# Hybrid encoder layers: sliding attention in units of one chunk and two heads per group, f32r scores, rotary swaps by transfers, the mix split by token chunk

## What is computed

```python
u = rmsnorm(h, norm_g)
sb_q, sb_k, sb_v, sb_g, sw_q, sw_k, sw_v, sw_g = split(u @ w_in)       # 1024 x 3328
sb_o = stick_breaking_attention(sb_q, sb_k, sb_v) * silu(sb_g)         # 8 heads of 64, causal
qr, kr = rope(sw_q), rope(sw_k)                                        # 8 query heads, 2 key heads
sw_o = sliding_window_gqa(qr, kr, sw_v, sinks) * silu(sw_g)
h = h + concat(sb_o, sw_o) @ w_out                                     # 1024 x 1024
```

## Time and profile before

| | us |
|---|---|
| three runs, median | 1393.2 |
| lowest, highest | 1391.79, 1398.45 |
| profiled execution, its own time | 1392.5 |
| its span | 1390.7 |

### The profile page before, as it was taken

How to read it: one execution, slowest core, us unless ns; L and a number is a source line. 1 busy time by engine, 2 the same in 40 slices (tenths; PEclk the granted TensorE clock), 3 DMA queues, 4 the chain that set the end, 5 groups by cost and what they waited for, 6 DMA issues and landing times.

```text
span 1390.7 us, 23502 instructions
## 1 busy us (share of the span) xinstructions
PE 1274.6 (92%) x9314; PEld 1162.3 (84%) x9314; DVE 819.4 (59%) x1560; ACT 450.9 (32%) x1239; POOL 235.3 (17%) x96
## 2 busy tenths in 40 slices
PE   4699999999898999979979999999989899997996
PEld 3598888988787888869969898888878788886995
DVE  5926555464766777652392664546475677765327
ACT  4313333233243333331131333333324333333113
POOL 1421111011010010232142111011101101023211
PEclk7699999999999999989999999999999999997998
DMA  4511110111001110031311111011100010103103
GB/s 160 192 46 31 31 32 16 31 31 32 16 17 23 25 24 24 31 123 47 138 61 46 31 31 29 19 31 31 27 21 16 16 31 16 32 31 120 50 16 121
DMA packets 96075, 64.24 MB, mean 46 GB/s; under 512 B 35920, under 2 KB 89424, under 8 KB 95968
## 3 DMA queue, kind: packets, MB, share of 16 engines
q1 hardware_dynamic: 94960, 61.22, 14.6%
q10 hardware_dynamic: 864, 1.35, 0.3%
q0 software_dynamic: 144, 0.18, 0.1%
HBM read 50.21 MB, written 12.71 MB: 45 GB/s over the span
## 4 chain that ended last, share of the span: by engine, by line
PE 75%; DVE 15%; issue 5%; ACT 3%; POOL 1%; DMA 0%; SPq 0%; DVEq 0%; ACTq 0%; POOLq 0%
PE psum L605 34%; PE psum L610 16%; PE psum L661 6%; PE psum L690 5%; PE psum L673 5%; DVE dvT L1172 3%; DVE mix L1068 2%; PE psum L726 2%; DVE X L1248 2%; PE psum L754 1%; PE psum L728 1%; PE psum L757 1%; DVE small L1245 1%; PE psum L722 1%; PE psum L739 1%
## 5 line engine op out<-in xcount | busy, mean ns | idle before, releaser
L605 PE MATMUL psum<-UH,WH 128*128 128x344 f32 (+1 forms) x1632 | 548.5, 336 | 21.2 <-DVE UL L1075 8.3
L605 PE MATMUL psum<-UL,WH 128*128 128x344 f32 (+1 forms) x1632 | 532.8, 327 | 0.0
L610 PE MATMUL psum<-UH,WL 128*128 128x344 f32 (+1 forms) x1616 | 523.9, 324 | 0.4 <-POOL WL L1358 0.4
L605 PEld LDWEIGHTS psum<-UH,WH 128*128 128x128 f32 x1632 | 314.9, 193 | 40.0 <-issue 15.6
L1358 POOL TENSOR_TENSOR WL<-w_raw,WH 128x1024 fp32r<-128x1024 f32 x68 | 174.2, 2563 | 1024.1 <-DVE WH L1116 1024.1
L605 PEld LDWEIGHTS psum<-UL,WH 128*128 128x128 f32 x1632 | 314.4, 193 | 0.4
L610 PEld LDWEIGHTS psum<-UH,WL 128*128 128x128 f32 x1616 | 309.4, 191 | 1.4 <-POOL WL L1358 1.4
L1193 DVE TENSOR_TENSOR_SCAN X<-X,stick 16x16 f32<-16x16 f32 (+5 forms) x144 | 123.9, 903 | 29.6 <-ACT X L956 29.4
L966 ACT ACTIVATE PT<-psum 128x512 f32<-128x512 f32 (+6 forms) x328 | 130.9, 440 | 22.3 <-PE psum L673 11.4
L956 ACT ACTIVATE X<-psum 128x264 f32<-128x264 f32 (+9 forms) x240 | 91.2, 432 | 82.8 <-PE psum L661 82.6
L1196 DVE TENSOR_TENSOR_SCAN X<-X 128x352 f32<-128x352 f32 (+4 forms) x96 | 94.7, 1027 | 29.5 <-ACT X L956 29.5
(11 more groups left out here) (129 smaller groups left out, 1498.1 us busy)
## 6 DMA issues: line engine op xcount, KB each, us to landing
w_raw<-in_w_in SPq DMA_DIRECT2D x36, 512.0 KB, 3.7
h_spill<-X SPq DMA_DIRECT2D x16, 520.0 KB, 5.1
X<-h_spill SPq DMA_DIRECT2D x16, 520.0 KB, 5.2
w_raw<-in_w_in SPq DMA_DIRECT2D x32, 256.0 KB, 3.7
w_raw<-in_w_out SPq DMA_DIRECT2D x16, 256.0 KB, 2.8
w_raw<-in_w_out SPq DMA_DIRECT2D x32, 128.0 KB, 3.3
out<-X SPq DMA_DIRECT2D x6, 512.0 KB, 4.2
mix<-in_x SPq DMA_DIRECT2D x3, 512.0 KB, 5.6
```

Of the source, the lines that this page charges most:

```text
L605: pe.matmul(bank[:, 0:width], WH[:, j % 2, k, :], u[:, k, chunk_uses(c)], start=(k == 0 and u is UH), stop=False)
L610: ins = pe.matmul(bank[:, 0:width], WL[:, j % 2, k, :], UH[:, k, chunk_uses(c)], start=False, stop=(k == KT - 1))
```

## The change

- **Units.** Sliding attention goes by 18 units (`UNITS`): half hp (two query heads of each group) and range r (two chunks of 64 tokens; one unit for the meta tokens). Within a unit, query columns are ordered by chunk and head, 128 of them for one chunk and two heads, against exactly 144 keys (meta, chunk before, own chunk), laid out in `SKH`, `SKL` as 16 groups of 80 columns. There is no mask.
- **Scores** are three f32r products each (queries and keys split in high and low), each of 64 partitions, one group on each half; both score banks belong to one unit.
- **Rotary.** ACT copies the projection to `dvT`, SP swaps the halves by four SBUF to SBUF transfers into `vT`, DVE has three operations on 128 partitions, one task later; high parts (ACT) and low parts (POOL) come another task later.
- **Order.** Values first, then `sk`, `sq 0`, `sq 1` fill the fourth stick stage; then `sg 0`, `sg 1`, `sq 2`, `sq 3` and, in the second nine units, `sg 2`, `sg 3`. A unit's steps are ST (main and meta part), SZ of n+2, SAV of n-1, SD of n+1.
- **Mix.** `split` goes by token piece and by rows (0 to 3 with POOL's low part, 4 to 5 and 6 to 7 with DVE's). Gates of half 0 are applied where DVE reads the values; half 1 is gated by piece. Two output products of the first piece are made ahead of SAV 14 and SAV 16 (`EARLY_OUTS`); their addition is a step of its own.
- **Pieces** are 400, 384 and 256 tokens. Reloads of `h` start by row as rows come free. The values' projection and the half-1 gates need no factor 0.5 any more; it is in the copy of the values.

```diff
-CHUNKS = [(0, 352), (352, 344), (696, 344)]
+CHUNKS = [(0, 400), (400, 384), (784, 256)]
-P_RING = 4
-REST_RING = 4
+P_RING, P_SLOT = 3, 688
+REST_RING = 3
...
-WEIGHT = dict(Z=1.5, T=0.6, R=0.0, AV=0.6, AV_rest=0.15, SZ=1.0, SD=0.3, ST=0.7, SAV=0.5, gate=0.0)
-OUT_ORDER = [0, 2, 1, 3, 4, 5, 6, 7]
+WEIGHT = dict(Z=1.0, T=0.6, R=0.0, AV=0.6, AV_rest=0.15, SZ=0.7, SD=0.0, ST=0.4, SAV=1.0, gate=0.0, split=0.0)
+OUT_ORDER = [4, 5, 6, 7, 2, 3, 0, 1]
+EARLY_OUTS = {(0, 0): ("SAV", 14), (1, 0): ("SAV", 16)}
+META_UNIT = 8
+UNITS = [(hp, r) for hp in range(2) for r in (0, META_UNIT, 1, 2, 3, 4, 5, 6, 7)]
+HALF = len(UNITS) // 2
...
+    def delayed(tasks):
+        out = [list(task) for task in tasks] + [[], []]
+        for i, task in enumerate(tasks):
+            for step in task:
+                if step[0] == "proj" and ORDER[step[1]][0] in ("sk", "sq"):
+                    e = rope_tile(*ORDER[step[1]][:2])
+                    out[i + 1].append(("rope_add", e, step[2]))
+                    out[i + 2] += [("rope_high", e, step[2]), ("rope_low", e, step[2])]
+        return out
+    def swa_fill():
+        tasks = proj("sv", 0) + proj("sk", 0) + proj("sq", 0) + proj("sq", 1)
+        tasks[3] += [("turn_sv", 0), ("turn_sv", 1), ("turn_sv", 2)]
+        tasks[4] += [("turn_sv", 3), ("turn_sv", 4)]
+        for kind, s in (("sg", 0), ("sg", 1), ("sq", 2), ("sq", 3), ("sg", 2), ("sg", 3)):
+            tasks += proj(kind, s)
+        return delayed(tasks)
...
+        for n in range(first, last):
+            out += [("ST", n, part) for part in (("main", "meta") if UNITS[n][1] != META_UNIT else ("meta",))]
+            if n + 2 < len(UNITS):
+                out.append(("SZ", n + 2))
+            out += lagged([], [("SAV", n)])
+            if n + 1 < len(UNITS):
+                out.append(("SD", n + 1))
...
+    steps += [("SZ", 0)] + window[12] + lagged([], []) + window[13] + [("SZ", 1), ("SD", 0)] + flat(window[14:18])
+    steps += merge(swa_attention(0, HALF), window[18:24], 0.3, 1.2)
+    late = merge(swa_attention(HALF, len(UNITS)), window[24:], 0.5, 1.5) + lagged([], [])
+    for n, (hp, r) in enumerate(UNITS):
+        c = unit_chunk(r)
+        if hp == 1 and n + 1 == units_until(1, c):
+            at = max(late.index(("SAV", n)), late.index(("proj", TILE_OF["sg", 3], c))) + 1
+            late[at:at] = [("gate", c), ("split", c, 2)]
+    for c in range(3):
+        at = late.index(("proj", TILE_OF["sg", 3], c)) + 1
+        late[at:at] = [("split", c, 0), ("split", c, 1)]
...
+                def swap(e, c):
+                    sp.wait_ge(raw_in.sem, raw_in.at(l, 3 * e + c + 1))
+                    if e == 0:
+                        sp.wait_ge(turned.sem, turned.at(l, TURN_AT["turn_sv", 4] + 1))
+                    for a in range(0, 128, HD // 2):
+                        other = a ^ (HD // 2)
+                        sp.dma_start(swapped_of(c)[a:a + HD // 2, :], raw_of(c)[other:other + HD // 2, :])\
+                            .then_inc(raw_swapped[c].sem, 16)
...
+                    for u in range(unit_columns(n_unit)[0]):
+                        first, count, at = keys_of(r, u)
+                        a, rows_out = (0, 32) if r == META_UNIT else (32 + 128 * (2 * r + u), 128)
+                        for i, (low, keys) in enumerate(((0, keys_h), (0, keys_l), (1, keys_h))):
+                            for g in range(2):
+                                rows = slice(64 * g, 64 * g + 64)
+                                q = SQ[rows, 2 * hp + low, a:a + rows_out]
+                                z = z_bank[0:rows_out, g, 144 * u + at:144 * u + at + count]
+                                ins = pe.matmul(z, q, keys[rows, first:first + count], start=(i == 0), stop=(i == 2))
...
+                    link(dve.tensor_tensor(swapped_of(c), swapped_of(c), sinT[:, chunk_uses(c)], ALU.mult))
+                    link(dve.tensor_tensor(raw_of(c), raw_of(c), cosT[:, chunk_uses(c)], ALU.mult))
+                    dve.tensor_tensor(raw_of(c), raw_of(c), swapped_of(c), ALU.add).then_inc(rope_added.sem, 1)
...
+                    if units == 2:
+                        link(ins)
+                        both = unit_numbers(n_unit, 5).unsqueeze(2).unsqueeze(3).to_broadcast([nq, 4, 2, 64])
+                        ins = dve.tensor_tensor(window_bands(n_unit, 0), window_bands(n_unit, META), both, ALU.mult)
```

More of the change, by code:

```diff
@@ L156, in sb_attention, with swa_attention, merge @@
         return [(WEIGHT[step[0]], step) for step in out]
-    def swa_attention(s):
+    def swa_attention(first, last):
         out = []
[L161 to L173, removed]
+        for n in range(first, last):
[5 more added lines that the diff above has]
+                out.append(("SD", n + 1))
         return [(WEIGHT[step[0]], step) for step in out]
-    def merge(weighted, fill, lead):
+    def merge(weighted, fill, lead, pace=1.0):
         total, at, n, out = sum(w for w, _ in weighted), 0.0, 0, []
@@ L957, in stick_scores, with copy_turned @@
                                        ACT.Sigmoid, scale=-SCALE).then_inc(z_read.sem, 1)
-                def copy_turned(step, key, parts):
-                    use, slot = TURN_AT[step], PT_AT[key]
+                def copy_turned(step, rows, width):
+                    use, slot = TURN_AT[step], PT_AT[step]
                     act.wait_ge(turned.sem, turned.at(l, use + 1))
@@ L964, in copy_turned @@
                         act.wait_ge(av_done.sem, av_done.at(l, PT_LEFT[slot - PT_RING] + 1))
[L965 to L967 removed]
+                    act.activation(PT[0:rows, slot % PT_RING, 0:width], t_bank[use % T_RING][0:rows, 0:width], ACT.Copy)\
+                        .then_inc(pt_in.sem, 1)
@@ new lines, in window_scores @@
+                    use, nq, (units, w) = Z_AT[step], unit_rows(n_unit), unit_columns(n_unit)
+                    if n_unit >= P_RING:
+                        act.wait_ge(turned.sem, turned.at(l, LAST_TURN[PAIRS * BLOCKS + n_unit - P_RING] + 1))
+                    act.wait_ge(peaked.sem, peaked.at(l, n_unit + 1))
+                    low, diff, total = (unit_numbers(n_unit, i) for i in (1, 2, 3))
+                    act.activation(by_unit(diff, n_unit), by_unit(diff, n_unit), ACT.Exp).then_inc(sink_exp.sem, 1)
@@ new lines, in window_scores @@
+                    for g in range(2):
+                        for u in range(units):
+                            k, a = 2 * g + u, 64 if u == UNITS[n_unit][1] == 0 else 0
+                            ins = act.activation(window_weights(n_unit)[:, k, a:w],
+                                                 z_bank[0:nq, g, 144 * u + a:144 * u + w], ACT.Exp,
+                                                 bias=low[:, k:k + 1], scale=SCALE, accum_out=total[:, k:k + 1])
+                        ins.then_inc(z_read.sem, 1)
@@ L1235, in window_peak @@
-                    link(dve.scalar_tensor_tensor(out=m[:, 2:4], in0=m[:, 0:2], scalar=-SCALE, in1=sink,
+                    n_unit = step[1]
+                    use, nq, (units, w) = Z_AT[step], unit_rows(n_unit), unit_columns(n_unit)
+                    peak, low, diff = (by_unit(unit_numbers(n_unit, i), n_unit) for i in range(3))
+                    dve.wait_ge(z_full.sem, z_full.at(l, use + 2))
+                    scores = z_bank[0:nq, :, 0:units * w].rearrange("q g (u k) -> q g u k", u=units)
@@ L1314, in _ @@
                         gate_window(step[1])
-                    elif kind == "split_mix":
-                        split_mix(step[1])
+                    elif kind == "split" and step[2]:
+                        split_low(step)
                 assert chain.k == DVE_LINKS, f"dve links {chain.k}"
```

638 lines of the change are left out of this document (330 added, 308 removed).

## The result

The changed kernel takes **1480.8 us** (median of four runs, 1479.5 to 1483.2) where the kernel before took 1393.2 in the runs beside it (median of three, 1391.8 to 1398.5): a ratio of 1.062 (95% interval 1.058 to 1.066), slower by 6%. A fourth run of the kernel before took 1455.6 us, over 4% above its fastest, and is left out of the comparison as a slow run. The forecast was 1323, the range 1272 to 1366, and slower had been given a chance of 0.07.

The account below looks back on a forecast made before the run. TensorE's work, and DVE stretches it stands waiting for, were taken to bound the kernel. Per layer −22 − 3.5 − 1.5 − 4 − 7 + 5 = −33, both −66, ends −4: from 1392.5 to 1322.5, forecast 1323 us, range 1272 to 1366.

Parts of the forecast that it names:

- E: Sliding stage: uncovered units cost TensorE idle rounds, a projection piece hides the wait; with F plus 5 us a layer.
- F: Sliding stage: DVE and POOL exclude each other at the shared port; POOL's split parts cost 3.5 us.
- The ring: Sliding units' cycle of turn, score, peak, copy and weighing: 5.1 us a round, 2.4 of it TensorE idle without filling.
- The slower case: Whole kernel slower than before, chance 0.07, through weight loads not hidden behind the short piece: 1410 us.
- Rival 1: Sliding stage: the ring doesn't bind, DVE runs ahead; 19 us a layer go, 1285 us; chance 0.20.
- Rival 2: Sliding stage becomes a DVE stage, POOL's low parts and splits meet the ring: +38, 1361 us; chance 0.20.
- Rival 3: Matmuls with 256 columns: weight load isn't hidden, up to 0.053 us more each, 1410 us; chance 0.07.
- C: Projections with the new piece lengths: columns and count stay, so nothing is gained or lost if the fixed part stays fixed.
- A: Sliding scores: a unit of twelve f32r matmuls takes 1.0 us; minus 22 us a layer.
- B: Sliding transposes minus 3.5 us and values minus 1.5 a layer; fewer steps between kinds of work, minus 4.
- D: Rotary by swap transfers, mostly hidden: losses in the fourth stick stage fall from 15 to 8 us, minus 7 a layer.

Follow-up runs that it names:

- e1: Changed kernel with the weighing of unit n+1 put ahead of score n+2 and of the filling, and planner weights altered: 1359.1 us, ratio 0.976.
- e5: Changed kernel with only the planner's weights altered, so that fillings come in only behind the weighing: 1392.9 us, ratio 1.001.
- e6: e1 with the rotary's high and low parts placed ahead of what else is in their task: 1346.0 us.
- e9: e6 with the filling of the second nine units spread, at 1.1 instead of 1.5 times the needed pace: 1338.4 us.
- e12: e6 with the edits of e9 and e10 together, the second half's filling pace then set to 1.0: 1329.3 us, ratio 0.955.
- e2: Changed kernel with the low parts of the rotary and of mix rows 0 to 3 moved from POOL to DVE: 1485.9 us.
- e10: e6 with the low parts of the rotary and of the stick half of the mix moved from POOL to DVE: 1338.6 us.
- e3: Kernel before with pieces of 400, 384 and 256 tokens and the stick scores' planner weight 1.0 instead of 1.5: 1393.1 us, ratio 1.000.
- e7: e6 with DVE's low part of a split put one step ahead of POOL's: 1346.1 us.

## Why the prediction was wrong

**The step that failed is in E: "A projection piece behind the score hides the wait."** It counted which units have a piece, and priced those without. It did not ask which of DVE's steps stand between the piece and the weighing in the list. In all such units but two (0, which has no values to copy yet, and 5), DVE's copy of the values or a step that the piece brings does, and it can't start before TensorE has ended the piece: the cover is itself waited for. The term E + F was +5 a layer; of the 158 us between forecast and result, 122 come back when the weighing is put ahead (e1), 88 of them with the piece alone moved (e5). Another 13 were a wait that the prediction called hidden ("they stand a further task later"), POOL's low part of SQ behind a weight tile's (e6); 17 are uncovered units and POOL's low parts (e9 to e12), and 6 are left. The prediction had the sentence that would have caught it ("with gate, ACT copy and low part of piece 1 ahead of weigh 17, costs 5"), and used it for one unit only. There it was right: the turn of unit 17 waits 4.79 us (643.93). The longest wait, 12.28 us, is more than two rounds. The ring itself was sized well: in a unit without a piece a round takes 5.7 us (530.71 to 536.41) with 1.79 idle, where 5.1 and 2.4 were taken.

The slower case was given 0.07 and laid on the weight load; the likelier mechanism on that side, in plain sight in the list of steps, was not a rival. None of the three rivals came about:
- Rival 1 (the ring doesn't bind): no, neither in the changed kernel nor in e12, where 16 us are still waited for weighing.
- Rival 2 (port): not the main cause, since e1 takes 122 us away with the contacts in place, and e2 gains nothing. But contacts lengthen single waits (6.4 of the 12.28 us above). Once the order is right, e10 takes 7.4 us out of the two layers, against 38 that the rival had.
- Rival 3 (weight loads at 256 columns): no. Matmuls with 256 columns come every 0.117 us (592.30, 592.42, 592.53 in the timeline), with 384 every 0.176; a step of each of the three pieces adds up to 0.475 us, as in the kernel before, and e3 is 1.000. The term C, nothing, stands.

The other terms:
- **A** (−22). One unit's scores take 0.72 us (590.20 to 590.92), where 1.0 was taken, and 1.35 where the clock is at half (618.80 to 620.15). This gain was sized too small, by about 4.5 us a layer (16 × 0.28) at full clock.

```profile
590.20 0.34 PE L824 MATMUL psum<-SKH,SQ 64*128 64x144 f32 x2
...
590.92 0.64 PE L854 MATMUL psum<-PT,Vn 48*128 48x256 f32 x2
...
592.08 0.38 PE L710 MATMUL psum<-UH,WH 128*128 128x256 f32 x1
```

- **B** (−3.5 and −1.5; its own figures give −1.8 for the second). A unit's values take 1.16 us (590.92 to 592.08), where 0.97 was taken, and its six transposes 0.74 (457.53 to 458.27) for 0.66. Together that is about 4.3 us a layer less gain (16 × 0.27), so B's miss cancels A's.

```profile
457.53 0.60 PE L836 MATMUL psum<-ident,P_early 128*128 128x128 f32 x4
...
458.27 0.34 PE L824 MATMUL psum<-SKH,SQ 64*128 64x144 f32 x2
```

- **D** (−7). With four weight tiles the fourth stage takes about 88 us and is busy 81.88 of them (in e12, with 31 matmuls more in the same window, 86.14); the 5.2 us wait is gone. 86 had been forecast. DVE waits for a swap four times, 18.4 us in all, the longest 7.8 us (381.94), where some 4 were taken. The first sliding score waits 3.9 us (429.93) for POOL's low part, where 2 were taken.
- **F**. A 64-column weighing took 2.18 us beside POOL (604.46) and 0.22 elsewhere, as the earlier trace rows led one to expect; the Trainium skill, "SBUF — State Buffer", section "Who interferes with whom", has the two exclude each other, and the trace agrees. A contact is lost time only where the step is one that TensorE waits for: e7 removes one with next to no effect.
- **Clock.** The waits bring a second loss that E had at 1.3 us a layer. After the 3.25 us wait for the residual's addition (657.55, behind a window at 0.61) 384-column matmuls come every 0.32 us, the lower of the two levels, until 663.5, and every 0.176 from there on:

```profile
657.55 0.69 PE L710 MATMUL psum<-UH,WH 128*128 128x384 f32 x1 [3.25 <-DVE X L1246]
658.04 0.53 PE L710 MATMUL psum<-UL,WH 128*128 128x384 f32 x1
658.36 0.53 PE L715 MATMUL psum<-UH,WL 128*128 128x384 f32 x1
```

Between the profiles of the changed kernel and of e1 lie 121.5 us. TensorE's idle time falls by 83 of them (209.0 to 125.6 us), and its busy time by 38 (1270.4 to 1232.3) for the same 8824 matmuls, with the granted clock at 0.933 for 0.895. So about a third of what the order cost was not waiting but slower work beside the waits.

The parts of the sum that concern the work were nearly right. From the kernel before to e12, TensorE's busy time falls by 54 us (1274.6 to 1220.2), where A and B with their smaller steps had 62 in two layers, and e12 is 6 us from the forecast of 1323. That it comes so close is partly luck: A's and B's misses cancel, and e12 has edits that the forecast didn't have. The forecast was of the change's content; the kernel that was timed had an order that hid little of it.

## What to carry to other kernels

Where engines walk one list, a filling covers a wait only if nothing stands ahead of the awaited step on its engine that needs the filling itself or anything that comes behind it on the filled engine: write out the list around each wait, engine by engine, and ask of each entry when it can start. If all engines have idle time in the same stretch, look at the order before any single cost. A step's planner weight decides what stands ahead of it, so give the step that releases the critical engine the first place in its unit.

## What the runs showed of the hardware

- A contact between DVE and POOL can cost DVE more than twice its plain time (2380 against 992 ns for the same 128x800) and the kernel nothing; where moving low parts from POOL to DVE took contacts away from the changed kernel, it took 5 us more, with DVE busy as long as before.
- The four swaps of 50 KB landed 2.0 us after their issue in the median, where 3.3 us for 128 KB was the nearest row.

```profile
vT<-dvT SPq DMA_DIRECT2D x40, 50.0 KB, 2.0
```

- Twelve f32r products of a unit, on both halves of the rows, take 0.72 us where six took 0.54 in the earlier trace rows: the cost is not in proportion to their number in these two places.
